# A two-layer transformer with three attention branches: scores over compressed keys taken with the keys in the array, then turned back

## The reference

```python
def _compress(kv, pos_emb, w1, w2):           # 15 windows of 32 tokens, one vector each
    ...
    return jax.nn.gelu(flat @ w1) @ w2
...
s_c = jnp.einsum('bqgrd,bngd->bqgrn', qn, k_cmp) * scale
p_c = _masked_softmax(s_c, (cmp_last[None, :] <= tq[:, None])[None, :, None, None, :])
o_c = jnp.einsum('bqgrn,bngd->bqgrd', p_c.astype(v_cmp.dtype), v_cmp)
...
o = g[..., 0:1] * o_c + g[..., 1:2] * o_s + g[..., 2:3] * o_w
```

## Time and profile before

| | us |
|---|---|
| median of 3 runs | 1201.17 (1201.12 to 1202.13) |
| the profiled execution | 1201.98 |
| its span | 1200.3 |
| TensorE busy | 1190.6 |
| VectorE busy | 731.8 |
| ScalarE busy | 569.7 |
| granted TensorE clock | 0.999 of full speed |

### The profile page before, as it was taken

One profiled execution on the slowest core, in us unless ns is written; L12 is line 12 of the kernel. 1 busy time (PEld: TensorE's weight loads), 2 busy tenths in 40 slices (PEclk: granted clock), 3 DMA queues, 4 the chain that ended last, 5 costly groups with the idle time before them and its releaser, 6 DMA issues.

```text
span 1200.3 us, 16393 instructions
## 1 busy us (share of the span) xinstructions
PE 1190.6 (99%) x5885; PEld 976.3 (81%) x5885; DVE 731.8 (61%) x896; ACT 569.7 (47%) x735; POOL 30.6 (3%) x66
## 2 busy tenths in 40 slices
PE   8999999999999999999999999999999999999997
PEld 6888888888777888888888888888887788888886
DVE  5644546768878664444564554477688685554454
ACT  5434345446654354434453444454566445544433
POOL 2000000001000000000000000000000000000000
PEclk9999999999999999999999999999999999999999
DMA  7655554754335555655545555645643345655560
GB/s 263 229 175 199 185 187 144 242 188 158 106 105 176 176 175 183 202 175 188 179 169 203 196 185 176 207 148 182 200 169 106 109 142 170 230 190 175 191 211 36
DMA packets 148959, 210.99 MB, mean 176 GB/s; under 512 B 8128, under 2 KB 109104, under 8 KB 148912
## 3 DMA queue, kind: packets, MB, share of 16 engines
q1 hardware_dynamic: 148080, 209.51, 52.5%
q10 hardware_dynamic: 832, 0.84, 0.2%
HBM read 209.28 MB, written 1.05 MB: 175 GB/s over the span
## 4 chain that ended last, share of the span: by engine, by line
PE 98%; DMA 0%; DVE 0%; issue 0%; ACT 0%; SPq 0%; POOLq 0%; POOL 0%; DVEq 0%
PE ps L1227 30%; PE ps L1229 29%; PE ps L1228 29%; PE ps L1424 2%; PE ps L1313 2%; PE ps L1445 2%; PE ps L1474 1%; PE ps L1246 1%; PE ps L1363 1%; PE ps L1417 0%; DMA raw<-in_ffn_w_up_dram 0%; PE ps L1367 0%; PE ps L1380 0%; PE ps L1505 0%; PE ps L1400 0%; PE ps L1465 0%
## 5 line engine op out<-in xcount | busy, mean ns | idle before, releaser
L484 DVE TENSOR_TENSOR wlo<-raw,whi 128x2048 fp32r<-128x2048 f32 (+1 forms) x195 | 436.4, 2243 | 224.6 <-ACT whi L994 200.2
L1227 PE MATMUL ps<-whi,ht_hi 128*128 128x512 f32 (+1 forms) x1216 | 478.9, 394 | 1.1 <-DVE ht_lo L506 1.1
L1229 PE MATMUL ps<-whi,ht_lo 128*128 128x512 f32 (+1 forms) x1216 | 471.1, 387 | 0.0
L1228 PE MATMUL ps<-wlo,ht_hi 128*128 128x512 f32 (+1 forms) x1216 | 470.2, 387 | 0.0
L994 ACT ACTIVATE whi<-raw 128x2048 fp32r<-128x2048 f32 (+1 forms) x195 | 365.4, 1878 | 183.7 <-PE ps L1229 183.4
L1229 PEld LDWEIGHTS ps<-whi,ht_lo 128*128 128x128 f32 x1216 | 228.6, 188 | 47.9
L1227 PEld LDWEIGHTS ps<-whi,ht_hi 128*128 128x128 f32 x1216 | 228.9, 188 | 46.9 <-issue 2.6
L1228 PEld LDWEIGHTS ps<-wlo,ht_hi 128*128 128x128 f32 x1216 | 229.2, 188 | 44.0
L1227 PE MATMUL ps<-whi,at_hi 128*128 128x512 f32 x336 | 131.4, 391 | 0.0
L1229 PE MATMUL ps<-whi,at_lo 128*128 128x512 f32 x336 | 130.9, 390 | 0.0
L1228 PE MATMUL ps<-wlo,at_hi 128*128 128x512 f32 x336 | 130.8, 389 | 0.0
(11 more groups left out here) (164 smaller groups left out, 676.9 us busy)
## 6 DMA issues: line engine op xcount, KB each, us to landing
raw<-in_ffn_w_down_dram SPq DMA_DIRECT2D x88, 512.0 KB, 3.9
raw<-in_w_in_dram SPq DMA_DIRECT2D x88, 512.0 KB, 4.4
raw<-in_ffn_w_gate_dram SPq DMA_DIRECT2D x85, 512.0 KB, 3.7
raw<-in_ffn_w_up_dram SPq DMA_DIRECT2D x85, 512.0 KB, 4.7
raw<-in_w_out_dram SPq DMA_DIRECT2D x16, 512.0 KB, 4.0
raw<-in_w_branch_c_dram SPq DMA_DIRECT2D x8, 512.0 KB, 4.2
raw<-in_w_branch_b_dram SPq DMA_DIRECT2D x4, 512.0 KB, 4.1
raw<-in_w_branch_a_dram SPq DMA_DIRECT2D x4, 512.0 KB, 4.1
```

Source lines behind the costliest of these rows:

```text
L484: nc.vector.tensor_tensor(wlo[:, n, 0:w], raw[:, n, 0:w], whi[:, n, 0:w].bitcast(F32), ALU.subtract).then_inc(lo_done, 1)
L1227: nc.tensor.matmul(o, xh, wh, start=start, stop=False)
L1228: nc.tensor.matmul(o, xh, wl, start=False, stop=False)
L1229: return nc.tensor.matmul(o, xl, wh, start=False, stop=stop)
```

## The change

For C the keys stand in the array, 32 columns for two heads, and the queries move, 256 columns: four matmuls write 32 partitions each of bank 4, keys in rows and tokens in columns. ScalarE copies that to SBUF (`sc_t`), and TensorE turns it back with two transposes (`turn_scores`), put in after the first six matmuls of the slot's slab. The mask is no longer put in by TensorE: VectorE adds it, one add for each token tile, out of PSUM into `prob`, before the maxima. Of the index scores of token tile 1, three of four are done behind the slab's split and no longer ahead of the scaling of C. A dummy exponential ahead of the slots sets ScalarE's function table, which the exponential of C did before.

```diff
-V_STEPS = 224
+V_STEPS = 226
...
+        sc_t = w1_k[:, SEQ:2 * SEQ]
...
                 if pair == "C":
-                    sc = ps[:, 4, 0:256].rearrange("p (h c) -> p h c", h=16)
-                    step(nc.vector.tensor_reduce(nmax[:, b, :], sc, AX_X, ALU.max, negate=True))
+                    o = prob[:, b, 0:256].rearrange("p (h c) -> p h c", h=16)
+                    for t in range(NT):
+                        step(nc.vector.tensor_tensor(o[:, 8 * t:8 * t + 8], ps[:, 4, t * P:(t + 1) * P]
+                                                     .rearrange("p (h c) -> p h c", h=8),
+                                                     kmask_b[:, t, :].unsqueeze(1).broadcast_to([P, 8, CPAD]), ALU.add))
                     own(l)
-                    o = prob[:, b, 0:256].rearrange("p (h c) -> p h c", h=16)
-                    step(nc.vector.tensor_tensor(o, sc, nmax[:, b, :].unsqueeze(2).broadcast_to([P, 16, CPAD]),
+                    step(nc.vector.tensor_reduce(nmax[:, b, :], o, AX_X, ALU.max, negate=True))
+                    own(l)
+                    step(nc.vector.tensor_tensor(o, o, nmax[:, b, :].unsqueeze(2).broadcast_to([P, 16, CPAD]),
                                                  ALU.add), ("max", e, 0))
...
                     if e == 1:
-                        index_scores(l, 1)
+                        index_scores(l, 1, [0])
                     if e > 0 and k is not None:
                         scaled(l, k, 0)
...
                     if e > 0:
                         convert(l, S + 17 + e)
+                    if e == 1:
+                        index_scores(l, 1, [1, 2, 3])
...
                 convert(l, S + 17)
+                warm_up(ACT.Exp)
                 for e in range(len(SLOTS)):
...
+                    if k == 1:
+                        eng.wait_ge(cscores_ps, l + 1)
+                        nc.scalar.activation(sc_t, ps[:, 4, 0:SEQ], ACT.Copy).then_inc(cscores_out, 1)
                     if e > 0:
                         convert(l, S + 17 + e)
...
                 if pair == "C":
-                    for t in range(NT):
-                        nc.tensor.matmul(ps[:, 4, t * P:(t + 1) * P], ident_b[:, :],
-                                         kmask_b[:, t, :].unsqueeze(1).broadcast_to([P, 8, CPAD]),
-                                         start=t == 0, stop=False, skip_group_check=True)
-                        for j in range(4):
-                            ins = nc.tensor.matmul(ps[:, 4, t * P + 32 * j:t * P + 32 * j + 32],
-                                                   qn_t[:, j, t * P:(t + 1) * P],
-                                                   kc_t[:, j // 2, :, :].rearrange("p a c -> p (a c)"),
-                                                   start=False, stop=t == 1 and j == 3, skip_group_check=True)
-                    ins.then_inc(sc_ps, 1)
+
+                    for j in range(4):
+                        ins = nc.tensor.matmul(ps[32 * j:32 * j + 32, 4, 0:SEQ],
+                                               kc_t[:, j // 2, :, :].rearrange("p a c -> p (a c)"), qn_t[:, j, :],
+                                               start=True, stop=True, skip_group_check=True)
+                    ins.then_inc(cscores_ps, 1)
                     return
...
+            def turn_scores(l):
+
+                pe.wait_ge(cscores_out, l + 1)
+                for t in range(NT):
+                    ins = nc.tensor.transpose(ps[:, 4, t * P:(t + 1) * P], sc_t[:, t * P:(t + 1) * P], ident[:, :])
+                ins.then_inc(sc_ps, 1)
...
-                         halfway=compressed if e == 0 else None, at=3)
+                         halfway=compressed if e == 0 else (lambda: turn_scores(l)) if k == 1 else None,
+                         at=1 if k == 1 else 3)
```

More of the change, by code:

```diff
@@ L259, in build @@
         sc_ps = sem("sc_ps")
+        cscores_ps = sem("cscores_ps")
+        cscores_out = sem("cscores_out")
         exp_done = sem("exp_done")
@@ L706, in heads_rest, with index_scores @@
                 step(nc.vector.tensor_tensor(lo, ps[:, heads_bank(n), :], hi.bitcast(F32), ALU.subtract), ("heads", n))
-            def index_scores(l, t):
+            def index_scores(l, t, heads=range(4)):
                 dve.wait_ge(exp_done, l * 2 + 1)
                 wv = work[:, 0:P] if t == 0 else work[:, P:3 * P]
-                for h in range(4):
+                for h in heads:
                     own(l)
@@ L1051, in ffn @@
                 if f == 1:
-                    warm_up()
+                    warm_up(ACT.Silu)
                 eng.wait_ge(rstd_ready, (l * 3 + n) * 3 + 3)
@@ L1194, in mixer, with warm_up @@
                     convert(l, S + m)
-            def warm_up():
-                nc.scalar.activation(warm[:, :], mhalf[:, 0:1], ACT.Silu).then_inc(warmed, 1)
+            def warm_up(function):
+                nc.scalar.activation(warm[:, :], mhalf[:, 0:1], function).then_inc(warmed, 1)
             copied = []
             eng.wait_ge(setup_g, SETUP_WARM)
-            warm_up()
+            warm_up(ACT.Silu)
             for l in range(DEPTH):
```

## The result

Over 22 runs of each, the changed kernel takes 1203.79 us in the median (1202.51 to 1204.56) and the kernel before 1202.2 (1200.85 to 1203.08): a ratio of 1.0013, with a 95% interval of 1.0007 to 1.0018. The change makes the kernel slower by 1.6 us (0.8 to 2.2), less than the 0.2% set as the bound of "same", but clear of the noise. The forecast was 1201.6 in a range up to 1203.2; the time lies 0.6 above that range.

What follows compares the result with a forecast made beforehand. TensorE, busy 99% of the span, was taken to bound the kernel, with VectorE's chain setting slot 3 after the change. 1201.98 + 0.4 (2 x 0.18) - 0.8 gave 1201.6 us, range 1199.3 to 1203.2.

Steps and rivals of the forecast that it cites:

- TensorE's block: Scores of C on TensorE: four matmuls in column groups take 0.65 us instead of 1.86, 1.21 less.
- net saving: TensorE, per layer: 1.21 us saved less 0.30 for turns and slab restart, 0.91 if nothing waits.
- the wait: TensorE at the turns of slot 3 waits about 1.1 us for VectorE's scaled rows of B.
- ScalarE's copy: Scores of C copied by ScalarE by 286.4, one us to spare before TensorE's turns; no wait.
- The two turns: Two transposes on TensorE that turn the scores of C back: 0.21 us, plus 0.09 for the slab's restart.
- turn-taking column groups: Rival, chance 0.07: the score passes run one after another, the block takes 2.03 us, time 1204.3.
- weight loads paid in each round: Rival, chance 0.08: each of two score rounds pays its 0.11 us load; 0.40 a layer, time 1202.0.
- Moving three index scores behind the split changes the order, not the sum: VectorE: the move adds no work and lets the scaling of C come before the three scores.
- the +0.18 of the forecast: TensorE in slot 3 goes on 0.18 us later than before in each layer, upper part of +0.10 to +0.21.
- The first reader of C: VectorE's first operation on the scores of C starts at 287.80 instead of 287.38, 0.42 us later.
- The base: Time of the kernel before: median 1201.17 us; 0.8 taken off the profiled execution's 1201.98.
- The rival of no wait: Rival, chance 0.12: VectorE's chain is shorter than counted, TensorE keeps 2 x 0.91 = 1.8 us, time 1199.3.

Runs made afterwards that it cites:

- GpSimd held: Changed kernel, with GpSimd's second piece of gates started only when the index scores are done; ratio 1.0006 to the kernel before.
- both cures: Changed kernel, with the selection round of slot 1 moved to slot 4 and GpSimd held until the index scores are done; median 1200.4 us, ratio 0.9980.

## Why the prediction was wrong

**The mechanism was right.** TensorE's block was put at 0.65 (0.66 measured: 284.98 less the matmul of 284.09 and its 0.23), its net saving at 0.91 (0.92), the wait was placed in slot 3 behind VectorE's scaled rows (though almost all of it at the second turn, where the first took 0.53 of the 1.25), there was none in slot 4, and ScalarE's copy was in time. Of the chain's links, the handing over from VectorE cost 0.06 (put at 0 to 0.11), and ScalarE started the exponentials 0.12 less late than VectorE its maxima, as worked out (0.11). The two turns themselves were dearer in the forecast (0.21) than here (0.14, 286.47 to 286.61). The rivals of turn-taking column groups and of weight loads paid in each round are out: all eight passes lie between 284.41 and 284.98, 0.57 with the way out of them, where rounds that paid their loads would take 0.68 without it. The weight loads themselves, all eight, stand at the front, in the first 0.16:

```profile
284.41 0.16 PEld L1410 LDWEIGHTS ps<-prob,kc_t 128*32 128x32 f32 x8 [0.36 <-DVE scr L655]
```

The rule of TensorE: Matmul & The Clock Gate of the Trainium skill (Part 3, The mechanism), that a load overlaps a matmul in flight only in another row group, is not what these rows show: the loads of the second round are done while the first round is in flight in the same rows of the array. The same section does name a background weight buffer as a second way for a load to go ahead; which way these loads took, no row tells.

**The step that failed** is in the part on VectorE: "Moving three index scores behind the split changes the order, not the sum". It lengthened VectorE's work by 0.50 a layer against the kernel before, and by 0.57 against the same order with GpSimd held, because it put the index scores beside GpSimd, whose piece of gates I had not placed at all; the earlier end of the slab on TensorE brings that piece forward too (291.88, which is 17.23 from the first compression pass, against 18.16). With GpSimd held, D is 28.42, 0.18 above before, which is just the +0.18 of the forecast. So per layer 0.56 of the 0.74 was missed here, 1.1 us in all.

**The first reader of C** was put 0.42 late and was 0.51 late: a term too small by 0.09. Of this 0.06 is the hand-over from TensorE, taken as 0.05 where it was 0.11 again (the turns end at 286.85, the add starts at 286.96), and 0.03 is the end of the turns. The adds were right (0.51 forecast, 0.52). That the +0.18 of the forecast came out with GpSimd held is in part luck. VectorE was then 0.96 late at the maxima of B, against 0.93 forecast, because the new order by itself saves 0.07 of what the later reader costs:

```profile
297.45 1.82 DVE L665 TENSOR_REDUCE nmax<-ps 128x4 f32<-128x512 f32 x2
```

This is 20.63 from the first compression pass (276.82 there), against 19.67 before. And the weight load behind the wait, which I had charged to come from +0.10 to +0.18, cost nothing at the second turn (302.78 to 303.63 is 0.85, as in the earlier trace rows); a hand-over of 0.06 and 0.02 more of delay stood in its place.

**The base** is the other half of the miss, too low by 1.0 us: the forecast stands on the median of three runs, 1201.17, and 22 runs of the same kernel give 1202.2. Subtracting 0.8 from the profiled execution put the forecast on the fast end of a spread of 2.2 us that the three runs did not show. 1.03 from the base and 2 x 0.56 from the missed term are 2.15 of the 2.19 us between forecast and measurement. Either alone would have stayed in the range.

**The rival of no wait** was given 0.12 and is what both cures make of the kernel; what separates it from the change is VectorE's place, not TensorE's work, as the sum had it.

## What to carry to other kernels

A saving on the engine that bounds the kernel is kept only as far as the producers of its next inputs are ahead of it: write down the slack of each hand-over within a slot or two behind the edit, and add the new work of the producer and the saving of the consumer to it before believing the gain. Here 0.66 us of slack (302.97 less 302.25 and a hand-over of 0.06) met 1.4 of delay and 0.92 of saving, and moving one independent piece of 1.2 us into a later idle stretch turned D from 0.74 above the kernel before to 0.48 below it. When work is moved on VectorE, look at what GpSimd does at the new place as well, not only at the order and sum on VectorE itself.

## What the runs showed that I had not expected

The start of the kernel moves by up to 2 us from run to run, more than the whole change. In the execution of the earlier trace rows the first slab's matmuls of 512 columns stand 0.43 apart, which is the lower of TensorE's two levels (512 columns at 1.2 GHz), for six or seven steps, and 0.23 apart afterwards; the granted clock in the profile's windows reads 1.00 in that stretch all the same. Timeline of TensorE before, and then of the changed kernel, in which no step is slow:

```profile
8.04 0.77 PE L1227 MATMUL ps<-whi,ht_hi 128*128 128x512 f32 x1 [1.07 <-DVE ht_lo L506]
8.60 0.63 PE L1228 MATMUL ps<-wlo,ht_hi 128*128 128x512 f32 x1
9.03 0.63 PE L1229 MATMUL ps<-whi,ht_lo 128*128 128x512 f32 x1
...
11.16 0.42 PE L1228 MATMUL ps<-wlo,ht_hi 128*128 128x512 f32 x1
...
11.65 0.40 PE L1227 MATMUL ps<-whi,ht_hi 128*128 128x512 f32 x1
```

```profile
7.96 0.47 PE L1240 MATMUL ps<-whi,ht_hi 128*128 128x512 f32 x1 [0.85 <-DVE ht_lo L509]
8.27 0.40 PE L1241 MATMUL ps<-wlo,ht_hi 128*128 128x512 f32 x1
8.51 0.39 PE L1242 MATMUL ps<-whi,ht_lo 128*128 128x512 f32 x1
```

In other profiles of the same start the slow stretch has 0, 8 or 11 such steps, and the first compression pass comes between 274.65 and 276.82 us. Ahead of these matmuls TensorE had been idle for 0.5 to 1.1 us. With the two matmuls on zeros in that gap the profile of the kernel with both cures has three slow steps, where without them it had none; that of the kernel before has none, where it had six or seven. They narrowed the runs as told above. That the gap decides it is suggested by the runs and not shown: the length of the gap doesn't order the profiles (after 0.85 us idle in the changed kernel no step is slow, after 0.56 in the one with GpSimd held 11 are), and the stretch may differ between executions of one kernel, of which one profile each was taken.
